# The masks of the first and the third layer: added by VectorE together with the row maxima instead of by TensorE, and the exponentials taken one step earlier on ScalarE

## What is computed

```python
def masked_softmax(s, mask):
    s = jnp.where(mask, s, -jnp.inf)
    m = jnp.max(s, axis=-1, keepdims=True)
    e = jnp.where(mask, jnp.exp(s - m), 0.0)
    return e / jnp.maximum(jnp.sum(e, axis=-1, keepdims=True), 1e-30)

# first layer (dsa_mixer, fox_mixer): 8 heads over keys picked per query, 8 heads with a
# forget decay under the causal mask
# third layer (nsa_mixer): 16 query heads, for each a selected and a windowed branch
# (both plain causal at 256 tokens) and a compressed one
```

## Time and profile before

| | before |
|---|---|
| median of 3 runs | 922.86 us |
| profiled execution: its time, its span | 921.05 us, 919.2 us |
| TensorE busy | 902.2 us, 98% of the span |
| VectorE busy | 648.4 us, 71% |
| ScalarE busy | 513.6 us, 56% |
| GpSimd busy | 133.0 us, 14% |
| first layer's attention stage | about 87.5 to 122 us of the span |
| third layer's attention stage | about 378 to 442 us of the span |

### The profile page before, as it was taken

The page is one execution under the profiler, slowest core; times in us unless marked ns, Lnnn a source line. Parts: engine busy times, 40 slices in busy tenths (PEclk is TensorE's granted clock), DMA queues, the critical chain, the costliest instruction groups (busy, mean ns, idle before and its releaser), DMA issues. The chain is left out here.

```text
span 919.2 us, 14875 instructions
## 1 busy us (share of the span) xinstructions
PE 902.2 (98%) x4853; PEld 753.0 (82%) x4853; DVE 648.4 (71%) x1175; ACT 513.6 (56%) x1019; POOL 133.0 (14%) x190
## 2 busy tenths in 40 slices
PE   8999999999999999999999999999999999999998
PEld 7878788888888878898888888888887788878876
DVE  4769656666666679866567666666887878777785
ACT  6654546544544466566454454454556666666573
POOL 3310200000000010245310000000430400400401
PEclk9999999999999999999999999999999999999999
DMA  9644024655555556400246555555464344454431
GB/s 365 224 141 163 19 93 139 207 197 190 186 192 193 183 170 208 151 1 1 94 148 211 190 188 191 193 183 189 154 206 155 127 154 162 155 176 150 160 115 47
DMA packets 40521, 146.39 MB, mean 159 GB/s; under 512 B 4496, under 2 KB 4752, under 8 KB 40464
## 3 DMA queue, kind: packets, MB, share of 16 engines
q1 hardware_dynamic: 40176, 145.43, 47.6%
q10 hardware_dynamic: 288, 0.21, 0.1%
HBM read 144.57 MB, written 1.05 MB: 158 GB/s over the span
## 5 line engine op out<-in xcount | busy, mean ns | idle before, releaser
L450 DVE TENSOR_TENSOR wl<-raw,wh 128x1024 fp32r<-128x1024 f32 x269 | 330.3, 1232 | 138.2 <-ACT wh L445 132.5
L445 ACT ACTIVATE wh<-raw 128x1024 fp32r<-128x1024 f32 x270 | 284.5, 1057 | 152.8 <-PE acc L347 132.3
L345 PE MATMUL acc<-wh,xhl 128*128 128x512 f32 (+1 forms) x472 | 191.9, 407 | 1.4 <-DVE wl L450 1.4
L347 PE MATMUL acc<-wh,xhl 128*128 128x512 f32 (+1 forms) x472 | 184.3, 391 | 0.0
L346 PE MATMUL acc<-wl,xhl 128*128 128x512 f32 (+1 forms) x472 | 183.8, 389 | 0.0
L345 PEld LDWEIGHTS acc<-wh,xhl 128*128 128x128 f32 x472 | 88.7, 188 | 24.8 <-issue 6.2
L347 PEld LDWEIGHTS acc<-wh,xhl 128*128 128x128 f32 x472 | 88.6, 188 | 19.3
L346 PEld LDWEIGHTS acc<-wl,xhl 128*128 128x128 f32 x472 | 88.8, 188 | 17.3 <-issue 1.0
L345 PE MATMUL acc<-wh,hh 128*128 128x512 f32 x256 | 100.8, 394 | 0.0
L346 PE MATMUL acc<-wl,hh 128*128 128x512 f32 x256 | 100.4, 392 | 0.0
L347 PE MATMUL acc<-wh,hl 128*128 128x512 f32 x256 | 100.1, 391 | 0.0
(11 more groups left out here) (318 smaller groups left out, 1333.3 us busy)
## 6 DMA issues: line engine op xcount, KB each, us to landing
raw<-stream SPq DMA_DIRECT2D x270, 512.0 KB, 3.3
h<-x SPq DMA_DIRECT2D x2, 512.0 KB, 4.7
out<-h SPq DMA_DIRECT2D x4, 256.0 KB, 2.1
row<-rows SPq DMA_DIRECT2D x1, 700.0 KB, 11.8
probs<-sel SPq DMA_DIRECT2D x1, 512.0 KB, 10.6
cst<-consts SPq DMA_DIRECT2D x1, 507.0 KB, 9.8
col<-cols ACTq DMA_DIRECT2D x1, 138.5 KB, 5.5
cst<-consts ACTq DMA_DIRECT2D x1, 64.0 KB, 4.3
```

The lines of the kernel that those rows point to most:

```text
L345: nc.tensor.matmul(out_, ah, bh, start=start, stop=False, skip_group_check=True)
L347: return nc.tensor.matmul(out_, al, bh, start=False, stop=stop_, skip_group_check=True)
L445: nc.scalar.activation(wh[:, u % SPLIT, :], raw[:, u % RAW, :], ACT.Copy).then_inc(w_hi, 1)
L450: nc.vector.tensor_tensor(wl[:, u % SPLIT, :], raw[:, u % RAW, :], wh[:, u % SPLIT, :].bitcast(F32), ALU.subtract).then_inc(w_lo, 1)
```

## The change

VectorE adds the mask itself: `masked_peak` computes `-(scores + mask)` into `probs` in SBUF and its minimum, the negated row maximum, into `nb`, for each of the four tiles. ScalarE's `Exp` then works in place in `probs` with scale -1. So the scores' PSUM banks are free once the maxima are taken (TensorE now waits for `s_peaked` where it waited for `s_exped`), while VectorE may write `probs[:, st % 2]` only once both `turn_p` of step `st-2` are done (`s_turned`, which the exponentials waited for before). TensorE's mask matmuls go, with the two copies `mskr` and `causr`. ScalarE takes `exponentials(it)` in iteration `it` instead of `exponentials(it-1)`; the evacuation at `it` = 1 now stands ahead of them.

```diff
-            def causal(bank, t):
-                return mm(bank[:, :, t * P:(t + 1) * P], idr[:, :], mskr[:, :, :], start=False, stop=True,
-                          skip_group_check=True)
...
             def ab_scores(st):
                 if st >= 2:
-                    pe.wait_ge(s_exped, 2 * (st - 1))
-                if st == FOX:
-                    pe.wait_ge(picked_set, 1)
+                    pe.wait_ge(s_peaked, 2 * (st - 1))
...
-                for a in range(2):
-                    mm((pair, acc)[a][st % 2][:, 0:KEYS], idr[:, :], (causr if st < FOX else picked)[:, :],
-                       start=True, stop=False, skip_group_check=True)
...
             def c_scores(n):
...
-                for t in range(T):
-                    causal(banks[t], t).then_inc(s_scored, 1)
...
             def exponentials(st):
-                if st >= 2:
-                    act.wait_ge(s_turned, 2 * (st - 1))
...
-                        src = ab_bank(st, a, t) if st < STEPS_AB else c_bank(st, t)[:, a * n:(a + 1) * n]
-                        last = s_.activation(pb[:, c0:c0 + n], src, ACT.Exp,
+                        last = s_.activation(pb[:, c0:c0 + n], pb[:, c0:c0 + n], ACT.Exp, scale=-1.0,
...
-            for it in range(1, STEPS_C + 2):
+            for it in range(STEPS_C + 2):
                 if 0 <= it - 2 < STEPS_C:
                     p_first(STEPS_AB + it - 2)
-                if it - 1 < STEPS_C:
-                    exponentials(STEPS_AB + it - 1)
...
+                if it < STEPS_C:
+                    exponentials(STEPS_AB + it)
...
+            def masked_peak(st, a, t, src, mask):
+                n = (t + 1) * P
+                c0 = t * 2 * P + a * n
+                return v_.tensor_tensor_reduce(probs[:, st % 2, c0:c0 + n], src, mask[:, t * P:t * P + n], -1.0, 3.4e38,
+                                               ALU.add, ALU.min, c_stat(nb, st)[:, a, t:t + 1])
+
             def peaks(st):
+                dve.wait_ge(s_turned, 2 * (st - 1))
                 for t in range(T):
                     dve.wait_ge(s_scored, 2 * st + t + 1)
-                    v_.tensor_reduce(c_stat(nb, st)[:, :, t], c_bank(st, t).rearrange("p (a k) -> p a k", a=2),
-                                     AX.X, ALU.max, negate=True).then_inc(s_peaked, 1)
+                    n = (t + 1) * P
+                    for a in range(2):
+                        last = masked_peak(st, a, t, c_bank(st, t)[:, a * n:(a + 1) * n], caus)
+                    last.then_inc(s_peaked, 1)
...
             def ab_peaks(st):
+                if st >= 2:
+                    dve.wait_ge(s_turned, 2 * (st - 1))
+                if st == FOX:
+                    dve.wait_ge(picked_set, 1)
...
-                    v_.tensor_copy(mskr[:, :, :], caus[:, 0:P].unsqueeze(1).broadcast_to([P, 2, P])).then_inc(masks_set, 1)
-                    v_.tensor_copy(causr[:, :], caus).then_inc(masks_set, 1)
```

More of the change, by code:

```diff
@@ L229, in program @@
         decay = sb("decay", [P, SEQ], F32R)
-        picked = sb("picked", [P, KEYS], F32R)
+        picked = sb("picked", [P, KEYS])
         idr = sb("idr", [P, P], F32R)
-        mskr = sb("mskr", [P, 2, P], F32R)
-        causr = sb("causr", [P, KEYS], F32R)
         hr = sb("hr", [P, 2, SEQ])
@@ L934, in ab_scores @@
                 if st >= 2:
[L935 to L937 removed]
+                    pe.wait_ge(s_peaked, 2 * (st - 1))
                 q, k = (B_QB + st, B_KB + st) if st < FOX else (B_QA + st - FOX, B_KA + st - FOX)
[L939 to L942 removed]
+                if st < FOX:
+                    for a in range(2):
                         for t in range(T):
[L944 removed]
+                            mm(ab_bank(st, a, t), selr[:, 2 * st + a, :], decay[:, 0:(t + 1) * P], start=t == 0,
                                stop=False, skip_group_check=True)
@@ L949, in ab_scores @@
                         last = mm(ab_bank(st, a, t), QK[rows, q, t * P:(t + 1) * P], QK[rows, k, 0:(t + 1) * P],
-                                  start=False, stop=True, skip_group_check=True)
+                                  start=st >= FOX, stop=True, skip_group_check=True)
                         if t == T - 1:
@@ L1125, in c_scores @@
                     for part in range(2):
-                        mm(banks[t], c_q(n)[:, 0, t * P:(t + 1) * P], c_keys(n % CG, part)[:, :, 0:(t + 1) * P],
-                           start=part == 0, stop=False, skip_group_check=True)
-                for t in range(T):
-                    causal(banks[t], t).then_inc(s_scored, 1)
+                        last = mm(banks[t], c_q(n)[:, 0, t * P:(t + 1) * P], c_keys(n % CG, part)[:, :, 0:(t + 1) * P],
+                                  start=part == 0, stop=part == 1, skip_group_check=True)
+                    last.then_inc(s_scored, 1)
             def c_values(n):
@@ L1196, in first_steps @@
                 if uu == 2:
-                    pe.wait_ge(masks_set, 2)
+                    pe.wait_ge(masks_set, 1)
                     pe.wait_ge(q_hi, 8)
@@ L1557, in _ @@
                     keys_out(9, QK[:, B_KB:B_KB + 2, :])
-            for it in range(1, STEPS_AB + 2):
+            for it in range(STEPS_AB + 2):
                 if 0 <= it - 2 < STEPS_AB:
                     p_first(it - 2)
-                if it - 1 < STEPS_AB:
-                    exponentials(it - 1)
+                if it == 1:
+                    evac(act, G_VB, U_ABO, 0, Y[:, 0, BV:BV + GW], rr(N_A0), GW)
+                if it < STEPS_AB:
+                    exponentials(it)
                 if it >= STEPS_AB:
                     act_turn_block(act, 1, ccs=(it - STEPS_AB,))
-                if it == 1:
-                    evac(act, G_VB, U_ABO, 0, Y[:, 0, BV:BV + GW], rr(N_A0), GW)
             act.sem_inc(z_act, 2)
@@ L1966, in ab_peaks @@
                     for t in range(T):
-                        last = v_.tensor_reduce(c_stat(nb, st)[:, a, t:t + 1], ab_bank(st, a, t), AX.X, ALU.max,
-                                                negate=True)
+                        last = masked_peak(st, a, t, ab_bank(st, a, t), caus if st < FOX else picked)
                     last.then_inc(s_peaked, 1)
```

14 lines of the change are left out of this document (4 added, 10 removed).

## The result

| | before | after |
|---|---|---|
| median | 923.45 us (4 runs, 922.78 to 924.11) | 940.63 us (4 runs, 936.0 to 944.22) |
| ratio, 95% interval | | 1.0191 (1.017 to 1.0213) |
| profiled execution: its time, its span | 921.05 us, 919.2 us | 938.38 us, 936.6 us |
| start of the last `misc` matmuls of the third layer's attention | 445.30 us of the span | 460.73 us |

What follows compares the result with a forecast made beforehand. A loop through VectorE (scores, maxima, copy, transposes) was taken to bound the attention steps, level with TensorE's own work in the third layer; the terms summed to +10.5 us, forecasting 933.4 us, range 927 to 939.

Steps and rivals of the forecast that it cites:

- I leave TensorE's clock out: Both attention stages: no clock term, as every slice is at full speed and new waits are 0.6 us per plain step.
- Plain steps: Attention steps without extra work: 3.66 us each, +3.1 us over five in the third layer, +0.6 over four in the first.
- the rows: Profile rows of the same masked instruction in the second block: a step's maxima take 1.22 us, against 0.94 and 1.07.
- the masks' time is hidden behind `p_first`: Both attention stages: scores lie beside `p_first` (1.05 and 1.13 us, below 1.19), so taking masks off TensorE shortens nothing.
- rival 1: Both attention stages: TensorE stays the bound and the masks' 8.1 us are won, 914.8 us; chance 0.05.
- The opening: Third layer's start: exponentials of step 1 stand ahead of the first `p_first`, 2.0 us later; +2.2 us with the next step.
- with `q_high`: Steps `it` = 4 and 6: `q_high` behind the running step's exponentials holds `p_first`; about +1.0 us each, +2.0 together.
- `it` = 9: Third layer: the compressed branch's `Exp` comes behind the exponentials and delays VectorE, 5.1 us where 3.81; +1.3 us.
- `it` = 12: Third layer: the two copies to `o_tok` hold the next `p_first`; +0.9 us.
- The first layer: First layer's attention: four steps of picked heads +0.6 us, opening +1.1, last two steps without maxima 0.3 saved.
- Rival 2: Loop closes, but ScalarE's extra work doesn't hold it: only plain steps and half the openings, +5.3 us, 928.2; chance 0.15.
- Rival 3: Masked maxima paid in full, 1.74 us: 0.52 more in some 17 loop-ruled steps, +8.8 us, 942.2; chance 0.08.

Runs made afterwards that it cites:

- number 2: After with ScalarE's old order (exponentials of step it-1 in iteration it), masks and maxima still on VectorE: 926.93 us median, ratio 1.005.
- number 5: After with the mask matmuls kept on TensorE, so the mask is added twice: 940.87 us median, ratio 1.0194.
- number 6: After with dummy matmuls of zeros in TensorE's waits of the third layer's loop: 936.41 us median, ratio 1.0145.
- number 11: number 9 with VectorE's first copy of the first layer moved ahead of the two instructions that make `picked`: 919.06 us median, ratio 0.996.
- number 12: number 9 with seven matmuls of zeros in TensorE's wait for the first layer's first copy, the copy left in place: 919.07 us median, ratio 0.9953.
- number 8: After with ScalarE's old order and VectorE's copy of `ptp` ahead of the maxima in every step: 919.97 us median, ratio 0.9976.
- number 9: number 8 with `probs` three deep, so VectorE's wait for the second transposes goes too: 919.92 us median, ratio 0.9987.
- number 10: Before with only VectorE's copy of `ptp` put ahead of the maxima, masks still on TensorE: 922.03 us median, ratio 0.9993.
- number 4: Before with one wait added: VectorE's maxima wait for both transposes of step it-2 (`s_turned`): 925.92 us median, ratio 1.0035.
- number 1: The changed kernel run again, nothing altered: 942.49 us median, ratio 1.0217.

## Why the prediction was wrong

**The step that failed is the sentence "I leave TensorE's clock out".** It rested on one row: before waits 1.47 us at 98.07 and keeps its clock there. That a single wait did no harm in one execution says little: in number 2 the same place with 1.9 us of waiting was followed by half speed, and the changed kernel waits in nearly every step, not once. A longer wait of before, 2.25 us up to 728.53, did no harm either, and the same one (2.38 us) was followed by half speed in after.

What the runs showed in its place is a term of 7.3 us, give or take 2.5: the clock takes 9.7 us from the median of after (940.63 against 930.9) and 2.4 from that of before (923.45 against 921.0). Before had some of it already: the 1.8 us that the prediction adds between the profiled execution, at a clock of 1.0, and the median fit its line, 7.3 us per 0.01, at 0.998.

The Trainium skill (TensorE: Matmul & The Clock Gate, A second HAM failure mode: psum-queue depth-cycling) describes a matmul kernel whose groups are parted by short idle times again and again, with a clock that swings between its two levels. That would have been a rival here. The trace of after agrees as far as the swings go (five stretches in the profiled execution); that the number of short waits makes them, no run here shows. A price was to be had only from the changed kernel's own rows: 0.989 mean clock over 936.6 us is 20.6 us at half speed, and by the line above (930.9) they cost 7.5 us of the 938.4, 0.36 us for each.

The sum was made at full clock, and there it holds: after stands 9.9 us over before (930.9 and 921.0, give or take 2.5), forecast +10.5. The gap between the medians is this 9.9 and the 7.3 of clock.

- Plain steps: 3.53, 3.54 and 3.60 us in the third layer where the clock was full, forecast 3.66; 3.71 in the first. In the first the maxima took 1.11 and not 1.22, but the scores last 1.31 from the first to the second transposes and not 1.19: I took `p_first` for the longer, and it was not. Two errors that nearly cancel. In the third layer the scores took 1.23 and the maxima 1.12. On the maxima of the first layer the estimate from the Trainium skill (VectorE: DVE Perf Modes, The TRN2 errata), no change there, was nearer than mine (1.07 before, 1.11 after). In the third, 0.94 became 1.12, +0.18, where it gave +0.25 and the rows +0.28: both too much.
- That the masks' time is hidden behind `p_first` (number 5), and so rival 1 in vain: right for the third layer. In the first, where the scores are the bound, keeping them adds 0.35 to a step.
- The opening: `p_first` 2.1 later beside what came before it, forecast 2.0 for it; second transposes 3.41 behind the first. The step, 384.74 to 390.60, is 1.9 longer than before's. Right in place, and it is also where the clock of the third layer first fell, which was not in its price.
- The steps with extra work, from first transposes to first transposes, all at full clock: with `q_high` 401.39 to 407.52 and 411.12 to 416.87, 0.9 and 1.0 more than before, forecast 1.0 each; `it` = 9 (425.93 to 431.11) 5.18 against 3.81, forecast +1.3; `it` = 12 (440.69 to 445.32) +0.8, forecast 0.9; the last pair 0.4 less, as forecast. All right.
- The first layer: its last first transposes come 1.3 later (120.56 for 119.30), forecast 0.6 + 1.1 - 0.3 = 1.4. Of this the opening is 0.8 (102.80 for 102.04), less than the 1.1 forecast, and the four steps are 0.7.
- Rival 2 (ScalarE's order doesn't hold the loop) is refuted by number 2: that order alone is 7 us at full clock. My terms for it were 2.2 + 2.0 + 1.3 + 0.9 + 1.1 = 7.5.
- Rival 3 named 942.2, near the median, for the wrong reason: the maxima were not paid in full in any row.

What stays open is what makes the clock fall. Filling one wait or shortening it took away the stretch behind it in the profiled execution (numbers 6, 11, 12; one execution each), and the versions that wait least keep most of the clock (0.988 to 1.0 in numbers 8 to 12, 0.976 to 0.992 in after). But stretches also began behind waits of 0.4 us (numbers 4 and 12), in other places from run to run, and before's wait of 2.25 us had none, so no single wait can be priced.

## What to carry to other kernels

Where a change puts short waits on TensorE in step after step, ask for the clock as a term of its own and widen the range upward, even if every slice of before is at full speed. Then look at each in-order queue: here the masked maximum was not the trouble, and its wait for the buffer was one only because a copy TensorE waits for stood behind it (3.9 us in number 4, 0.5 between numbers 8 and 9); the other was that ScalarE took an optional piece of work ahead of one that others wait for. With both put in order the same idea goes from 1.9% slower to 0.2% faster (number 8), and with a third buffer and the earlier copy to 0.4% (number 11).

## What I had not expected of the hardware

The clock's cost is nearly linear over whole runs, 5.6 to 8.2 us per 0.01 of mean clock in every version, so a handful of runs with their clocks separates schedule from clock, if some of them are near 1.0: the bounds are 0.2 to 0.7 us where they are, and 1.2 to 5 where they are not. The scatter itself is a sign: ten runs of after spread over 12 us, 56 of before over 4. And the clock can stay at 1.2 GHz while TensorE's rows show it busy without a gap: 388 to 392 and onward to 401 in number 12, and 390 to 406 in the profile of number 1.
